# Main attention's scores: one head's long multiplications beside the other head's short ones, in two phases

## The reference, cut to what matters

```python
BRANCHES = ((128, 1), (512, 4), (2048, 16))      # window, dilation
def dilated_branch(q, k, v, window, dilation):   # query t attends to t, t-d, ..., t-window
    ...
    s = jnp.einsum("brhnqd,brhnkd->brhnqk", qb, kk).astype(jnp.float32)
    s = jnp.where(mask, s, NEG_INF)
    m = jnp.max(s, axis=-1)
    p = jnp.exp(s - m[..., None])
    l = jnp.sum(p, axis=-1)
    o = jnp.einsum("brhnqk,brhnkd->brhnqd", p, vv.astype(jnp.float32)) / l[..., None]
    ...
```

## Time and profile before

| what | value |
|---|---|
| time, median of 3 runs | 1077.89 us (1077.33 to 1078.76) |
| the profiled execution's own time | 1078.67 us |
| its span | 1076.6 us |
| PE busy with matmuls | 1069.7 us, 99% of the span |
| PE weight loads | 970.5 us, 90% |
| DVE / ACT / POOL busy | 805.5 / 647.9 / 54.3 us |
| what the DMA engines moved | 195.65 MB, mean 182 GB/s |
| PE's share of the chain that ended last | 88% |
| granted PE clock | 9 tenths or more in each slice (mean 1.00) |

### The profile page before, as it was taken

The page is one execution under the profiler, slowest core; times in us unless marked ns, Lnnn a source line. Parts: engine busy times, 40 slices in busy tenths (PEclk is TensorE's granted clock), DMA queues, the critical chain, the costliest instruction groups (busy, mean ns, idle before and its releaser), DMA issues.

```text
span 1076.6 us, 19507 instructions
## 1 busy us (share of the span) xinstructions
PE 1069.7 (99%) x7424; PEld 970.5 (90%) x7424; DVE 805.5 (75%) x1221; ACT 647.9 (60%) x976; POOL 54.3 (5%) x47
## 2 busy tenths in 40 slices
PE   9999999999999999999999999999999999999998
PEld 8998888888898999999889888889999989999987
DVE  5986877875588787887878788637796778888960
ACT  6446746464487777777676465535464757656650
POOL 0000000000000000000000000000200111222300
PEclk9999999999999999999999999999999999999999
DMA  8565665777286676652447658753454664565760
GB/s 256 175 204 187 204 211 172 230 253 240 64 230 173 183 201 185 173 158 81 134 145 222 209 163 272 260 157 99 138 166 142 195 211 130 184 194 178 234 234 20
DMA packets 219789, 195.65 MB, mean 182 GB/s; under 512 B 9881, under 2 KB 195277, under 8 KB 219725
## 3 DMA queue, kind: packets, MB, share of 16 engines
q1 hardware_dynamic: 219369, 194.55, 58.3%
q10 hardware_dynamic: 356, 0.22, 0.1%
HBM read 191.85 MB, written 1.05 MB: 179 GB/s over the span
## 4 chain that ended last, share of the span: by engine, by line
PE 88%; DVE 6%; ACT 2%; DMA 2%; SPq 1%; issue 1%; DVEq 0%; ACTq 0%
PE ps L831 21%; PE ps L902 9%; PE ps L734 8%; PE ps L735 8%; PE ps L736 8%; PE ps L679 7%; PE ps L680 7%; PE ps L681 7%; DVE w_lo L1856 3%; PE ps L846 2%; PE ps L844 2%; PE ps L845 2%; DMA raw<-in_conv_w_in 1%; ACT w_hi L1357 1%; PE ps L945 1%; PE ps L748 1%
## 5 line engine op out<-in xcount | busy, mean ns | idle before, releaser
L1856 DVE TENSOR_TENSOR w_lo<-raw,w_hi 128x1024 fp32r<-128x1024 f32 (+1 forms) x298 | 398.8, 1382 | 51.1 <-ACT w_hi L1357 50.0
L1357 ACT ACTIVATE w_hi<-raw 128x1024 fp32r<-128x1024 f32 (+1 forms) x298 | 331.3, 1156 | 112.8 <-PE ps L736 38.6
L679 PE MATMUL ps<-x_both,w_hi 128*128 128x256 f32 x656 | 187.0, 285 | 0.4 <-DVE w_lo L1856 0.2
L681 PE MATMUL ps<-x_both,w_lo 128*128 128x256 f32 x656 | 185.6, 283 | 0.0
L680 PE MATMUL ps<-x_both,w_hi 128*128 128x256 f32 x656 | 185.6, 283 | 0.0
L831 PE MATMUL ps<-x_both,w_hi 128*128 128x512 f32 x640 | 149.4, 390 | 0.0
L831 PEld LDWEIGHTS ps<-x_both,w_hi 128*128 128x128 f32 x640 | 118.7, 188 | 24.4 <-DVE w_lo L1856 0.7
L679 PEld LDWEIGHTS ps<-x_both,w_hi 128*128 128x128 f32 x656 | 125.8, 192 | 2.1 <-issue 1.3
L680 PEld LDWEIGHTS ps<-x_both,w_hi 128*128 128x128 f32 x656 | 125.9, 192 | 0.0
L681 PEld LDWEIGHTS ps<-x_both,w_lo 128*128 128x128 f32 x656 | 125.8, 192 | 0.0
L734 PE MATMUL ps<-w_hi,a_hi 128*128 128x512 f32 x296 | 115.7, 391 | 0.0
(11 more groups left out here) (260 smaller groups left out, 1693.8 us busy)
## 6 DMA issues: line engine op xcount, KB each, us to landing
raw<-in_ffn_w_gate_up SPq DMA_DIRECT2D x80, 512.0 KB, 5.2
raw<-in_w_up SPq DMA_DIRECT2D x44, 512.0 KB, 4.5
raw<-in_ffn_w_down SPq DMA_DIRECT2D x24, 768.0 KB, 5.9
raw<-in_conv_w_in SPq DMA_DIRECT2D x24, 512.0 KB, 5.0
raw<-in_w_q SPq DMA_DIRECT2D x48, 256.0 KB, 4.9
raw<-in_w_kv SPq DMA_DIRECT2D x48, 256.0 KB, 4.2
raw_v<-in_w_kv SPq DMA_DIRECT2D x48, 256.0 KB, 3.8
raw<-in_w_in SPq DMA_DIRECT2D x20, 512.0 KB, 4.5
```

Of the source, the lines that this page charges most:

```text
L679: nc.tensor.matmul(o, wh[:, k0 + k, c], hi[:, k, :], start=(k == 0), stop=False)
L681: ins = nc.tensor.matmul(o, wl[:, k0 + k, c], hi[:, k, :], start=False, stop=(k == kt - 1))
L1357: nc.scalar.activation(w_hi[:, s, a * ph.cols:b * ph.cols], src, ACT.Copy)\
L1856: nc.vector.tensor_tensor(w_lo[:, s, c], src, w_hi[:, s, c], ALU.subtract)\
```

## The change

`score()` now has two helpers, `own(qt, hh)` with the four long multiplications of one query tile and head, and `dilated(hh)` with all 16 short ones of one head (both query tiles). It issues `own(1, 0)`, `dilated(1)`, `own(1, 1)`, `dilated(0)`, and then `own(0, 0)` and `own(0, 1)`. The multiplications themselves, their operands and their places in PSUM are the same 48; `scored` now goes up with the last one of `own(0, 0)` and of `own(0, 1)`. Nothing else in the program changes.

```diff
-                    for qt in range(2):
-                        own = P * (qt + 1)
+                    def own(qt, hh):
+                        w = P * (qt + 1)
                         for c in range(CLASSES):
...
+                            ins = nc.tensor.matmul(flat[m, o0:o0 + w], qkT[f, 0, q0:q0 + CB], qkT[f, 3, 0:w], start=True,
+                                                   stop=True, skip_group_check=True)
+                        return ins
+
+                    def dilated(hh):
+                        for qt in range(2):
+                            for g in (1, 2):
+                                for c in range(CLASSES):
...
+                                    nc.tensor.matmul(o, qkT[f, g, q0:q0 + CB], in_tiles(qkT[f, 3 + g, :])[:, :, c, :],
+                                                     start=True, stop=True, skip_group_check=True)
+
+                    for hh in range(2):
+                        own(1, hh)
+                        dilated(1 - hh)
+                    for hh in range(2):
+                        own(0, hh).then_inc(scored, 1)
```

More of the change, by code:

```diff
@@ L918, in score @@
                         pe.wait_ge(roped, q * 3 + 3)
-                    for qt in range(2):
-                        own = P * (qt + 1)
+                    def own(qt, hh):
+                        w = P * (qt + 1)
                         for c in range(CLASSES):
[L922 to L929, removed]
+                            f, m = slice(hh * HD, (hh + 1) * HD), slice(c * CB, (c + 1) * CB)
+                            q0, o0 = qt * P + c * CB, S_AT + hh * 1024 + qt * 512
+                            ins = nc.tensor.matmul(flat[m, o0:o0 + w], qkT[f, 0, q0:q0 + CB], qkT[f, 3, 0:w], start=True,
+                                                   stop=True, skip_group_check=True)
+                        return ins
@@ L930, in score @@
+                    def dilated(hh):
+                        for qt in range(2):
+                            for g in (1, 2):
+                                for c in range(CLASSES):
                                     f, m = slice(hh * HD, (hh + 1) * HD), slice(c * CB, (c + 1) * CB)
-                                    q0, o0 = qt * P + c * CB, S_AT + hh * 1024 + qt * 512 + own
+                                    q0, o0 = qt * P + c * CB, S_AT + hh * 1024 + qt * 512 + P * (qt + 1)
                                     o = flat[m, o0:o0 + P].rearrange("p (t g b) -> p t g b", t=2, g=2)[:, :, g - 1, :]
-                                    ins = nc.tensor.matmul(o, qkT[f, g, q0:q0 + CB], in_tiles(qkT[f, 3 + g, :])[:, :, c, :],
-                                                           start=True, stop=True, skip_group_check=True)
@@ L935, in score @@
-                                    if (qt, g, c) == (1, 2, CLASSES - 1):
-                                        ins.then_inc(scored, 1)
+                                    nc.tensor.matmul(o, qkT[f, g, q0:q0 + CB], in_tiles(qkT[f, 3 + g, :])[:, :, c, :],
[5 more added lines that the diff above has]
+                        own(0, hh).then_inc(scored, 1)
```

## The result

Over ten runs each, the changed kernel takes 1080.68 us (1079.9 to 1081.7), the kernel before 1078.43 us (1077.33 to 1079.47). The ratio is 1.0022 with a 95% interval of 1.0014 to 1.003: 2.3 us slower, by 1.5 to 3.2 us. The predicted time was 1080.6 us.

A forecast was written before the change was run, and what follows sets the result against it. PE was taken to bound the kernel. Eight blocks at +0.39 us give 3.1, less 0.4 for step 2's filled wait: +2.7 us on the median 1077.89, so 1080.6 us; range 1076.3 to 1081.6, the forecast's own 1079.8 to 1081.6.

The forecast's parts named there:

- What bounds the stretch: Score block, steps 3 to 8: PE, busy 99% of the span, passes any change of the block on one for one.
- The rule read from the two pauses: PE's queue in the score block: a multiplication begins only 0.03 us after the one 17 places ahead has ended; chance 0.60.
- The size of the term: Each of eight score blocks: +0.39 us, 1.91 for 1.52; eight give 3.1 us.
- starts keep the program's order: New score block: head 0's places, free since 0.46 us, get their first short multiplication only at 0.83 us.
- Steps 1 and 2: First two score blocks: +0.39 us each; step 2's 0.4 us PE wait is filled, step 1's 0.6 us wait absorbs nothing.
- Out of order: Rival, PE's queue: finished short multiplications make room, block 0.20 to 0.27 us shorter, program -1.2 to -1.6 us; chance 0.20.
- strict order of ends: Rival, score block: no multiplication ends before an earlier one, heads do not overlap; +0.65 us a block, +4.8 us; chance 0.08.
- some 6 us to spare: Loop step of 29.2 us: DVE works 23.1 us and ACT 22.2 us, so both have some 6 us free.

## Why the prediction was right

**What bounds the stretch** held. PE ran without a gap behind step 1 and six blocks passed their whole difference on. Clock and all the waits behind the block stayed as reckoned; `turn_p` has no wait ahead of it.

**The rule read from the two pauses** held in seven kernels, with block lengths of 1.52, 1.89, 1.68, 1.89, 1.44 and 1.65 us against 1.52, 1.86, 1.70, "1.9", 1.43 and 1.6 expected, and 1.89 against 1.91 in the change. Two pauses of different length in the old trace, each ending just behind the same event, were enough to give both the size and the event. What they could not tell, whether the queue frees from its head, the change itself decided: twelve short ones had ended by 406.56, and none of them let another in before 406.61. (The ends of PE's records are modelled. The rule does not rest on one of them: with 128-key ones at the head the pause ended earlier by as much as they are shorter.)

**The size of the term** was +0.39 us a block and measured +0.37. The small miss lies in the last eight multiplications: the last second pass was to start 1.72 us in, and starts 1.69 to 1.70 us in. Both pauses ended where they were reckoned, the first after 0.65 us, the second, reckoned at 1.35, between 1.34 and 1.36. Short passes (L935) by stretch, and long ones (L924) at the end:

```profile
405.99:407.33 1.34, 1.31 (x57) 1.00 0.97 287
405.99:407.35 1.36, 1.33 (x59) 1.00 0.96 285
```

```profile
405.99:407.68 1.69, 1.59 (x31) 1.00 0.93 276
405.99:407.69 1.70, 1.60 (x32) 1.00 0.93 277
```

One step of the working was wrong without costing anything: "starts keep the program's order". Head 0's first short one was to start at 0.83 us, behind head 1's last long one. Short passes, then long ones, by 406.77:

```profile
405.99:406.77 0.78, 0.75 (x33) 1.00 1.00 300
405.99:406.77 0.78, 0.71 (x9) 1.00 1.00 300
```

The first 32 short passes are head 1's, so the 33rd is head 0's first. It has begun within 0.78 us, while three of head 1's four long ones had still to start. A load or pass can go round an earlier one that waits for its place; it didn't go beyond the 64 in any run here.

**The time** came closer than the working earned. The 2.7 us were added to 1077.89, the median of three runs of the kernel before; over ten runs that median is 1078.43, 0.5 us higher, and the loss is 2.3 us, 0.4 us smaller. The two misses cancel. That 1080.6 stands against 1080.68 is luck; the working itself was off by 0.4 us.

**Steps 1 and 2** were to give 2 x 0.39 - 0.4 = +0.38 us. PE in order of time, the first score block and the projection of step 2, before:

```profile
320.42 0.45 PE L925 MATMUL ps<-qkT 64*32 64x128 f32 x16 [0.61 <-DVE v_tok L2141]
...
348.76 2.09 PE L902 MATMUL ps<-m_both,w_hi 128*128 128x512 f32 x8 [0.35 <-DVE v_tok L2141]
```

and after, from narrow windows:

```profile
320.08 0.41 PE L924 MATMUL ps<-qkT 64*32 64x256 f32 x3 [0.36 <-DVE v_tok L2147]
...
348.73 0.50 PE L902 MATMUL ps<-m_both,w_hi 128*128 128x512 f32 x1
```

That is 28.34 us before and 28.65 after, +0.31. The first block started 0.34 us earlier in the execution after; that lies ahead of everything the change touches and hides this part in the span. The sum is 6 x 0.37 + 0.31 = 2.5 us by the steps, 2.2 by the spans, 2.3 by the runs, and 2.7 was predicted.

**The rivals.** Out of order would have shown a block of about 1.2 to 1.3 us; strict order of ends about 2.1 with no short one under way early, while the 25 passes begun by 406.42 show that the places of the two heads do run side by side. (The Trainium skill, TensorEngine Tiling (Array Packing), Key Properties, is borne out for the places themselves; that the queue ahead of them binds them together stands in the trace, not there. The rule of the Trainium skill, TensorE: Matmul & The Clock Gate, The mechanism, that starts go strictly in program order, is not borne out: the 33rd short pass has begun by 406.77, and nine long ones only.)

**One reading was too generous.** From the busy sums I gave DVE and ACT "some 6 us to spare" a step. As a sum that is so, but the run with one-pass scores shows that with a block 0.57 us shorter PE already waits 0.3 us a step for DVE, because what counts is when DVE's copy can begin. It did not bear on this change, which lengthened the block; it would have spoilt a forecast of a large gain.

## What to carry to other kernels

When many small multiplications run side by side on PE, write their order so that those at the head of each run of 64 load and pass records end early and all places get equal work in turn; a slow one at the head stops the supply for places that stand empty. Before an order is changed to fill a resource, look in the old trace for a pause in the issue of instructions, ask which event it ends behind, and try that event on the new order. Moving 24 of the 32 short ones ahead of all long ones is what shortened the block here, by 0.09 us. And before a stretch is made shorter, look at what the next stretch waits for: here 0.95 us was the floor, and the one long wait behind it also cost clock.

## What the runs showed of the hardware that I had not expected

The limit is exact and counts records, not multiplications: the pass of the 33rd multiplication of two records and the start of the 18th of four came 0.03 us behind the end of the first, in each case looked at. Once the head has ended, new float32 multiplications follow 17 ns apart (in the changed kernel's order of time, long ones at 406.78, 406.79, 406.81). And passes of later multiplications start ahead of earlier ones that wait for their place, so PE's queue is neither strictly in order nor free: in all these traces it reorders inside the 64 and frees from the head.
